# Ten column groups of the input projection as block products, and ten adds moved to GpSimd

## The chip, the cores and the metric

One core of a Trainium2 chip runs one encoder block. The metric is device time in microseconds, the median of the runs shown. Everything is float32; matmuls take operands split into a high and a low part of type fp32r.

## The reference, cut to what matters

```
u = rmsnorm(x, g_mix)                       # x: 512 tokens x 2048
z = u @ W_in                                # 2048 x 6720 columns
qa, ka, va, cq, ckv, kr, ga, gb = split(z)  # 1024, 256, 256, 512, 512, 64, 2048, 2048
qa, ka: rmsnorm per head of 128, rotary; oa = softmax(qa ka^T / sqrt(128)) va; ya = oa @ w_a_out
latent branch from cq, ckv, kr: yb = ob @ w_b_out
h = x + (sigmoid(ga) * ya + sigmoid(gb) * yb) @ w_o
h += (silu(g) * u') @ w_down, [g, u'] = rmsnorm(h) @ w_gate_up
h += sigmoid(rmsnorm(h) @ w_ple_gate) * rmsnorm(p @ w_ple_proj); final rmsnorm
```

## The kernel before, in words

Activations lie with the feature on the partition and 512 tokens along the row. A matmul in full accuracy is three: high weights with high x, high weights with low x, low weights with high x (`product`). A *piece* (`piece`, L649) is 512 rows of a weight matrix by 256 columns: 1024 elements on a partition. SyncE loads it into one of four `raw` buffers (`load`, L390), ScalarE copies it to `w_hi` (`whi`, L1072, behind the use of the piece two before), VectorE subtracts to get `w_lo` (`wlo`, L1651), and TensorE runs 16 matmuls with the high part (L658) and 8 with the low part (L663). Four pieces are a *column group*, 256 columns of z: two 128x512 results in two PSUM banks, which VectorE scales by 1/rms of x while it empties them (`empty`, L1679, 128x1024).

Each engine has its own program, and each works strictly in the order written; the engines meet at semaphores. In the order of TensorE: the group of the keys (while x arrives), the group of the values with the total of the squares of x behind its second piece (`first_total`, L756), the four pieces of the rotary key (L762, 32 matmuls instead of 96), four groups of queries (the chains of two keys and the first query run beside the last three: square, total over the partitions with a matmul of ones, logarithm and exponential, a Newton step, gain, rotation, split), and then eight grouped-query heads.

The squares of x: ScalarE squares tile s into one of two buffers (`x_square`), VectorE adds it to `acc` (`x_add`, L1785), for s = 0 to 15, around the splits of pieces 4 and 5. Then ScalarE splits piece 6, copies the high part of the sum (`sum_split`), VectorE makes the low part (`sum_low`, L1720).

A head on TensorE (`gqa_head`, L784): scores (12 matmuls), two pieces of a gate group, the total of squares of the query three heads on (`head_total`), two pieces, transposes of the probabilities, four pieces of a second gate group with the weighing of the values between them. On ScalarE (L1221): table load, four exponentials, the square of the next query, splits of weight pieces, root, copies, and twice `gate_sigmoid` (L1208: sigmoid of a gate group and its store to DRAM). On VectorE (L1851): maxima, sums and scaling of the probabilities, low parts, norm and rotation of the query, emptying of the gate groups. The last head has two groups of the latent branch instead.

Later, the feed-forward part computes with 2x2 block products (`strassen`, L943): a *unit* is a product of a weight block with x by seven products of half size instead of eight. VectorE and one accumulating DMA make the sums of weight blocks, ScalarE snapshots intermediate banks between them. Units go in pairs, their products alternate. In a *wide* unit the products of high weights with high and low x are one matmul of 512 elements into two half banks, added up later (`folds`); in a *narrow* one they are two of 256. Per product: 8 (or 16) high matmuls (L977; L979 and L980) and 8 low ones of 256 (L983).

Of the kernel before, what the change touches and what calls it, by code (L numbers as in the profile page):

```python
# [25 lines left out]
F32 = mybir.dt.float32  # L26
# [32 lines left out]
N_QKV, N_KR, N_GATE = 0, 8, 28  # L59
N_LAT = N_GATE + 8 * 7  # L60
# [8 lines left out]
G_GATE = 7  # L69
G_LAT = G_GATE + 14  # L70
# [9 lines left out]
UNITS = FF + 24  # L80
A11, A21, A22, A12 = range(4)
# [52 lines left out]
def raw_count(v, i):  # L134

    return 16 * (v // 2) if raw_slot(v, i) in (4, 6) else 16 if v < 2 else 16 * (v // 2 + 1)
# [26 lines left out]

G_MIX, G_FFN, G_PLEN, G_POST, G_FIN, G_QA, G_KVA, G_QN, G_KN = 0, 16, 32, 48, 64, 80, 84, 88, 89
# [7 lines left out]
def build(nc, xT, pT, gains, tables, mats, w_in, w_qb, w_kvb, w_a, w_b, w_o, w_gu, w_dn, w_dn6, w_pg, w_pp,  # L172
          outT):
    with ExitStack() as ctx:
# [37 lines left out]
        sb("between", [P, 20, 2, SEQ])  # L212
# [7 lines left out]
        h_dram = nc.dram_tensor("h_dram", [KD, P, SEQ], F32, kind="Internal").ap()  # L220
        hid = nc.dram_tensor("hid", [3, 8, P, 8, 256], F32, kind="Internal").ap()
# [46 lines left out]
        kr_parts = sem("kr_parts")  # L268

# [30 lines left out]
        SQ_PARTS = r3[:, 7]  # L300
# [42 lines left out]
        X_HALF = [slice(0, 256), slice(256, 512)]  # L343

# [44 lines left out]
        def _(sp):  # L389
# [19 lines left out]
            n = 4  # L409
            for col in [C_V, C_KR, C_Q, C_Q + 256, C_Q + 512, C_Q + 768]:  # L410
                for j in range(4):
                    load(n + j, j, w_in, 4 * j, col)
                if n == 4:
                    sp.dma_start(tab[:], tables).then_inc(tables_in, 16)
                n += 4
            with sp.Fori(0, HEADS - 1) as h:
                ca, cb = sp.snap(h * COLS + C_GA), sp.snap(h * COLS + C_GB)
                for j in range(8):
                    load(h * 8 + N_GATE + j, j % 4, w_in, 4 * (j % 4), ca if j < 4 else cb)
# [37 lines left out]
            sp.wait_ge(gate_out[0], 16 * HEADS)  # L457
# [27 lines left out]
            sp.wait_ge(gate_out[1], 16 * HEADS)  # L485
# [154 lines left out]
        def _(pe):  # L640
# [43 lines left out]
            def head_total(m):  # L684
                pe.wait_ge(hsq_lo, m + 1)
                mm(ps[:, 7, :], ones_r[:], SQ_PARTS[:, 0, :], start=True, stop=False)
                mm(ps[:, 7, :], ones_r[:], SQ_PARTS[:, 1, :], start=False, stop=True).then_inc(htot, 1)

# [49 lines left out]
            def in_group(g, after=None, tiles=2):  # L738

                free(g)  # L740
                for j in range(4):
                    def tile_ready(k, j=j):
                        pe.wait_ge(u_lo, 4 * j + k + 1)

                    piece(4 * g + j, j, 2 * (g % 2), u_pieces(j), j == 0, j == 3, tiles,
                          tile_ready if g == 0 else None)
                    for step in (after or {}).get(j, []):
                        step()
# [13 lines left out]
            def rotary_key_group():  # L762
                free(2)
                for j in range(4):
                    pe.wait_ge(w_lo_done, N_KR + j + 1)
                    for k in range(4):
                        x, w = u_tile(4 * j + k), w_hi[:, j % HL, 0, k]
                        first, last = j == 0 and k == 0, j == 3 and k == 3
                        if last:
                            mm(ps[LOWER, 0, :], w[:, LOWER], x[:, 1, :], start=False, stop=False)  # L770
                        i = mm(ps[:, 0, :], w[:, 0:P], x[:, 0, :], start=first, stop=last)
                        if not last:
                            i = mm(ps[LOWER, 0, :], w[:, LOWER], x[:, 1, :], start=False, stop=False)
# [3 lines left out]
            in_group(3)  # L777
            pe.wait_ge(rstd_done, 1)
            in_group(4, {0: [lambda: head_total(0)], 3: [lambda: turn_v(res[:, 10, :], 4)]})
            in_group(5, {0: [lambda: head_total(1)], 3: [lambda: turn_v(res[:, 11, :], 5)]})  # L780
            in_group(6, {0: [lambda: head_total(2)]})


            def gqa_head(h, kv, more):  # L784
                b = h * 8 + N_GATE
                score(h, [Q_A], [K_A[kv]], h + 5)
                free(h * 2 + G_GATE)
                piece(b, 0, 2, u_pieces(0), True, False)
                piece(b + 1, 1, 2, u_pieces(1), False, False)
                if more:  # L790
                    pe.wait_ge(exp_done, h * 4 + 4)
                    head_total(h + 3)
                piece(b + 2, 2, 2, u_pieces(2), False, False)
                piece(b + 3, 3, 2, u_pieces(3), False, True)
                turn_p(h, 0, PT_BANK)
                turn_p(h, 1, PT_BANK)
                free(h * 2 + G_GATE + 1)
                piece(b + 4, 4, 0, u_pieces(0), True, False)
                weigh(h, 0, V_A[kv], PT_A)
                if more:  # L800
                    pe.wait_ge(hnorm, h + 4)
                turn_p(h, 2, PT_BANK)
                turn_p(h, 3, PT_BANK)
                piece(b + 5, 5, 0, u_pieces(1), False, False)
                weigh(h, 1, V_A[kv], PT_A)
                weigh(h, 2, V_A[kv], PT_A)
                weigh(h, 3, V_A[kv], PT_A)
                piece(b + 6, 6, 0, u_pieces(2), False, False)
                piece(b + 7, 7, 0, u_pieces(3), False, True)
# [4 lines left out]
            with pe.Fori(GROUP, HEADS - 1) as h:  # L814
                gqa_head(h, 1, True)
            gqa_head(HEADS - 1, 1, False)
# [251 lines left out]
        def _(act):  # L1068
# [3 lines left out]
            def whi(n, j):  # L1072
# [3 lines left out]
                if isinstance(n, int) and n >= LAST:  # L1076
                    act.wait_ge(piece_used, N_E + 4)
                    copy(as_piece(LAST_HI[j]), raw[:, j]).then_inc(w_hi_done, 1)
                    return
                if isinstance(n, int) and n == N_WO + 31:  # L1080
# [32 lines left out]
            def head_square(m, tile, need, count):  # L1113
                act.wait_ge(need, count)
                nc.scalar.activation(res[:, 13:14, :], tile, ACT.Square).then_inc(hsq, 1)
                act.wait_ge(hsq, m + 1)
                copy(SQ_PARTS[:, 0:1, :], res[:, 13:14, :]).then_inc(hsq_hi, 1)
# [1522 lines left out]
```

## Time and profile before

| | us |
|---|---|
| median of 3 runs (2668.5 to 2668.79) | 2668.55 |
| profiled execution, whole | 2669.43 |
| span of its instructions | 2667.6 |
| TensorE busy | 2650.6 |
| VectorE busy | 1906.9 |
| ScalarE busy | 1220.6 |
| GpSimd busy | 169.7 |

The span reaches from the first to the last instruction. Busy time is the union of an engine's instructions; a matmul's end is modelled, so neighbours overlap and the distance from start to start is the price of one.

### The profile page before, as it was taken

The numbers are of one execution on the slowest core, as the hardware profiler recorded it, in microseconds if no ns is written. First come the engines' busy times: TensorE is split into PE (matmuls) and PEld (weight loads), VectorE is DVE, ScalarE is ACT, GpSimd is POOL, SyncE is SP. The second block draws the span as 40 slices with busy tenths as digits, with TensorE's granted clock in tenths as the row PEclk, the third lists the DMA queues.
The fourth block names the chain that finished last, engine by engine and source line by source line (L and its number), as shares of the span: only waits on it lengthen the run. The fifth ranks groups of instructions, "written<-read, shape, count | busy, mean of one in ns | idle before, by whom it ended". The sixth has DMA issues, their size and how long they took to land. (4 is left out here: it accounts for less than half of the span.)

```text
span 2667.6 us, 37022 instructions
## 1 busy us (share of the span) xinstructions
PE 2650.6 (99%) x14596; PEld 2304.4 (86%) x14596; DVE 1906.9 (71%) x2192; ACT 1220.6 (46%) x1527; POOL 169.7 (6%) x130
## 2 busy tenths in 40 slices
PE   9999999999999999999999999999999999999998
PEld 7888888888888888898888888888899899999887
DVE  6555555455665433488998999998999898898745
ACT  5334344333554323355545545554555353454543
POOL 0000000010000111100000000000000000000052
PEclk9999999999999999999999999999999999999999
DMA  6333333333233454455455556545557654643332
GB/s 224 95 92 100 109 103 102 103 87 114 90 112 95 174 216 125 140 147 169 141 167 174 151 166 180 166 143 174 174 183 236 197 202 146 206 134 109 95 103 95
DMA packets 130434, 382.62 MB, mean 143 GB/s; under 512 B 11120, under 2 KB 37872, under 8 KB 127728
## 3 DMA queue, kind: packets, MB, share of 16 engines
q1 hardware_dynamic: 113824, 333.35, 37.7%
q0 software_dynamic: 9792, 34.61, 7.4%
q10 hardware_dynamic: 6672, 12.63, 1.2%
q8 instruction: 101, 1.65, 0.3%
q14 instruction: 45, 0.37, 0.0%
HBM read 301.90 MB, written 44.04 MB: 130 GB/s over the span
## 5 line engine op out<-in xcount | busy, mean ns | idle before, releaser
L1070 ACT ACTIVATE w_hi<-raw 128x1024 fp32r<-128x1024 f32 (+1 forms) x533 | 556.9, 1045 | 891.6 <-PE ps L663 447.0
L658 PE MATMUL ps<-arena,w_hi 128*128 128x512 f32 x3344 | 798.5, 390 | 0.4 <-DVE arena L1724 0.4
L658 PEld LDWEIGHTS ps<-arena,w_hi 128*128 128x128 f32 x3344 | 625.1, 188 | 133.0 <-issue 4.2
L1670 DVE TENSOR_TENSOR w_lo<-raw,w_hi 128x1024 fp32r<-128x1024 f32 x212 | 268.1, 1265 | 432.9 <-ACT w_hi L1070 432.4
L977 PE MATMUL ps<-arena,w_hi 128*128 128x512 f32 x1792 | 449.0, 392 | 0.5 <-DVE res L2248 0.5
L2060 DVE TENSOR_TENSOR w_lo<-raw,w_hi 128x1024 fp32r<-128x1024 f32 (+1 forms) x315 | 374.8, 1190 | 80.9 <-ACT w_hi L1070 79.3
L663 PE MATMUL ps<-arena,w_lo 128*128 128x512 f32 x1672 | 413.3, 389 | 0.0
L977 PEld LDWEIGHTS ps<-arena,w_hi 128*128 128x128 f32 x1792 | 322.2, 189 | 58.6 <-DVE res L2248 0.9
L663 PEld LDWEIGHTS ps<-arena,w_lo 128*128 128x128 f32 x1672 | 313.9, 188 | 65.1
L983 PEld LDWEIGHTS ps<-arena,w_lo 128*128 128x128 f32 x2468 | 332.3, 191 | 17.5
L983 PE MATMUL ps<-arena,w_lo 128*128 128x256 f32 x2468 | 346.3, 282 | 0.0
L1070 ACT ACTIVATE hi<-raw 128x1024 fp32r<-128x1024 f32 (+1 forms) x159 | 164.9, 1037 | 212.0 <-PE ps L983 207.9
L977 PE MATMUL ps<-arena,hi 128*128 128x512 f32 x896 | 224.4, 392 | 0.0
L2060 DVE TENSOR_TENSOR lo<-raw,hi 128x1024 fp32r<-128x1024 f32 (+1 forms) x157 | 187.0, 1191 | 41.3 <-ACT hi L1070 40.5
L977 PEld LDWEIGHTS ps<-arena,hi 128*128 128x128 f32 x896 | 161.1, 189 | 28.8
L983 PEld LDWEIGHTS ps<-arena,lo 128*128 128x128 f32 x1228 | 165.4, 191 | 8.7
L983 PE MATMUL ps<-arena,lo 128*128 128x256 f32 x1228 | 172.3, 282 | 0.0
L979 PE MATMUL ps<-arena,w_hi 128*128 128x256 f32 x676 | 166.3, 283 | 0.2 <-ACT res L1070 0.2
L980 PE MATMUL ps<-arena,w_hi 128*128 128x256 f32 x676 | 166.2, 283 | 0.0
L2510 POOL DMA_DIRECT2D raw<-raw x68 | 59.1, 869 | 1220.4 <-DMA raw<-w_gu 785.6
L979 PEld LDWEIGHTS ps<-arena,w_hi 128*128 128x128 f32 x676 | 129.7, 192 | 0.5 <-ACT res L1070 0.4
L980 PEld LDWEIGHTS ps<-arena,w_hi 128*128 128x128 f32 x676 | 129.8, 192 | 0.1
(206 smaller groups left out, 2645.4 us busy)
## 6 DMA issues: line engine op xcount, KB each, us to landing
raw<-w_gu SPq DMA_DIRECT2D x174, 512.0 KB, 4.1
raw<-w_in SPq DMA_DIRECT2D x108, 512.0 KB, 3.5
raw<-w_dn SPq DMA_DIRECT2D x64, 512.0 KB, 4.6
raw<-raw POOLq DMA_DIRECT2D x60, 512.0 KB, 7.3
hid<-res SPq DMA_DIRECT2D x22, 1024.0 KB, 4.8
raw<-w_o SPq DMA_DIRECT2D x32, 512.0 KB, 3.6
raw<-w_pg SPq DMA_DIRECT2D x32, 512.0 KB, 3.6
arena<-hid SPq DMA_DIRECT2D x14, 1024.0 KB, 8.3
```

Of the source, the lines that this page charges most:

```text
L658: mm(ps[:, bank + t, :], w_hi[:, s, t, k], x[:, part, :], start=first and k == 0 and part == 0, stop=False)
L663: i = mm(ps[:, bank + t, :], w_lo[:, s, t, k], x[:, 0, :], start=False, stop=last and k == len(xs) - 1)
L977: mm(parts, w, x[:, :, k], start=fresh and k == 0, stop=False, skip_group_check=not fresh)
L979: mm(out, w, x[:, 0, k], start=fresh and k == 0, stop=False, skip_group_check=not fresh)
L980: mm(out, w, x[:, 1, k], start=False, stop=False, skip_group_check=not fresh)
L983: i = mm(out, lo[:, k * P:k * P + P], x[:, 0, k], start=False, stop=k == pairs(v) - 1, skip_group_check=not fresh)
L1070: return nc.scalar.activation(out, in_, ACT.Copy, scale=scale)
L1670: tt(w_lo[:, j % HL], raw[:, j], w_hi[:, j % HL], ALU.subtract).then_inc(w_lo_done, 1)
L2060: tt(S_LO[s][:, columns(v)], operand(v, j), S_HI[s][:, columns(v)], ALU.subtract).then_inc(s_lo, 1)
L2510: pool.dma_start(RAWS[into][:, columns(v)], RAWS[more][:, columns(v)], accum_op=ALU.add).then_inc(sum_1_in[v % 2], 16)
```

## The change

Ten of the column groups (queries 4 to 7, gate A's first, gate B's first seven) become ten units of block products, between the rotary key and the rest. Two query groups follow (the seam, `N_SEAM`), then the heads with one group each: six of gate A in heads 0 to 5, the latent ones in heads 6 and 7. Units 0, 1, 8, 9 are narrow, 2 to 7 wide. The results of the units go to DRAM (`q_dram`, `gates`), as do the keys, values and the rotary key (`kv_dram`) until the seam. The four turned operands of x (T1 to T4) are made in `res` by VectorE from gained copies of x by ScalarE.

GpSimd adds the squares 6 to 15, and issues the ten accumulating DMAs of the units.

```diff
-N_QKV, N_KR, N_GATE = 0, 8, 28
-N_LAT = N_GATE + 8 * 7
+N_QKV, N_KR, N_SEAM, N_GATE = 0, 8, 12, 20
+N_LAT = N_GATE + 4 * 6
+Z_UNITS = 10
+def z_wide(v):
+    return 0 < v // 2 < Z_UNITS // 2 - 1
@@ tensor @@
             rotary_key_group()
-            in_group(3) ... in_group(6, {0: [lambda: head_total(2)]})
+            def z_product(v, j):
...
+                if j >= 4:
+                    pe.wait_ge(z_snap, snap_at(v, j - 4))
+                pe.wait_ge(z_hi, n + 1)
...
+            for a in range(0, Z_UNITS, 2):
+                for j in range(7):
+                    z_product(a, j)
+                    z_product(a + 1, j)
+            in_group(G_SEAM, {0: [first_seam_step], 2: [lambda: head_total(1)],
+                              3: [lambda: turn_v(res[:, 3, :], 5)]}, N_SEAM, 6)
+            in_group(G_SEAM + 1, {0: [lambda: head_total(2)]}, N_SEAM + 4, 2)
+            def gqa_head(h, kv, more, bank=2):
+                b = h * 4 + N_GATE
                 score(h, [Q_A], [K_A[kv]], h + 5)
+                pe.wait_ge(emptied, h + G_GATE)
+                piece(b, 0, bank, u_pieces(0), True, False)
                 if more:
                     head_total(h + 3)
+                piece(b + 1, 1, bank, u_pieces(1), False, False)
                 turn_p(h, 0, PT_BANK)
                 turn_p(h, 1, PT_BANK)
+                piece(b + 2, 2, bank, u_pieces(2), False, False)
                 weigh(h, 0, V_A[kv], PT_A)
                 turn_p(h, 2, PT_BANK)
                 turn_p(h, 3, PT_BANK)
                 weigh(h, 1, V_A[kv], PT_A)
+                piece(b + 3, 3, bank, u_pieces(3), False, True, before=last_weighs)
@@ scalar @@
             whi(5, 1)
             for k in range(11, 16):
                 x_square(k)
+            for k in range(8):
+                x_scale(k)
             whi(6, 2)
             sum_split(0)
             whi(7, 3)
             root(0, 7, 0, D)
+            z_turned_hi(T1_, 0, 1)
+            z_turned_hi(T1_, 1, 1)
+            for k in range(8, 16):
+                x_scale(k)
             whi(8, 0)
+            z_part(0)
             whi(9, 1)
+            nc.scalar.preload_act_table(ACT.Sigmoid)
...
+                for t in range(14):
+                    if 14 * q + t + 2 < 7 * Z_UNITS:
+                        z_part(14 * q + t + 2)
+                    if q == 0 and t in (7, 8):
+                        z_turned_hi(T3_, t - 7, 7)
...
+                    if t == 8:
+                        z_snap_s1(b)
+                        z_snap_row(b)
...
             def gqa_head(h, kv, more, latent=None):
                 ln_exp_table()
                 exps(h)
                 if more:
                     head_square(h + 3, res[:, bass.ds(h + 1, 1), :], hnorm, h + 3)
...
                 o_split(h, r3[:, bass.ds(h, 1), 0, :])
+                whi(b + 5, 1)
+                if latent is None:
+                    gate_sigmoid(h, 0)
@@ vector @@
             wlo(4, 0)
-            for s in range(6, 11):
-                x_add(s)
             wlo(5, 1)
-            for s in range(11, 16):
-                x_add(s)
+            z_t1(0)
+            z_t1(1)
...
             empty(K_KEPT, 0, 0, 3)
+            z_turned_low(T1_, 1)
             wlo(8, 0)
+            z_t2(0)
+            z_t2(1)
+            z_t4(0)
             wlo(9, 1)
             empty(V_KEPT, 2, 0, 7)
+            z_low(0)
             wlo(10, 2)
             wlo(11, 3)
...
+                        if t == 7:
+                            z_t3(0)
+                            z_t3(1)
...
                 o_split(h, r3[:, bass.ds(h, 1)])
+                if latent is None:
+                    gate_group(h, b + 3)
+                wlo(b + 5, 1)
@@ gpsimd @@
+            for s in range(6, 16):
+                add_square(s, 0, 0, sq_a)
+            for v in range(Z_UNITS):
+                into, more = z_slot(v, A21), z_slot(v, A22)
...
+                pool.dma_start(RAWS[into], RAWS[more], accum_op=ALU.add).then_inc(sum_1_in[v % 2], 16)
```

`x_scale(k)` copies tile k of x times its gain onto itself; `z_turned_hi` copies half of a turned operand (128x1024) to its high part; `z_part(n)` and `z_low(n)` split the weights of product n, a block of 128x1024; `z_snap_s1` copies a unit's first bank; `z_t1` to `z_t4` subtract parts of x (128x1024). The unit's products are numbered n = 14q + t, even t for the even unit of pair q.

## Rows read from the trace of the kernel before

**Rows 1.** The page, busy shares and 40 slices.
```profile
PE 2650.6 (99%) x14596; PEld 2304.4 (86%) x14596; DVE 1906.9 (71%) x2192; ACT 1220.6 (46%) x1527; POOL 169.7 (6%) x130
...
PE   9999999999999999999999999999999999999998
...
PEclk9999999999999999999999999999999999999999
```
**Rows 2.** Waits of TensorE: who waited for whom, us in total, times, longest.
```profile
PE ps L1056 <- ACT tab L1630: 2.2, 1, 2.2
```
**Rows 3.** Timeline of TensorE, first 110 us: start, length, instructions.
```profile
40.96 0.39 PE L681 MATMUL ps<-sum_r,ones_r 128*128 128x512 f32 x1
...
52.29 0.39 PE L771 MATMUL ps<-arena,w_hi 128*128 128x512 f32 x1
...
59.86 3.79 PE L658 MATMUL ps<-arena,w_hi 128*128 128x512 f32 x16
...
65.30 3.79 PE L658 MATMUL ps<-arena,w_hi 128*128 128x512 f32 x16
```
**Rows 4.** Chain that ended last, feed-forward part: start, us, what (wide, then narrow).
```profile
2096.53 1.84 PE ps L977 x8
...
2099.32 1.84 PE ps L977 x8
...
2140.52 0.96 PE ps L983 x8
...
2143.40 0.96 PE ps L983 x8
```
**Rows 5.** Timeline of ScalarE, first 110 us.
```profile
6.34 2.56 ACT L1070 ACTIVATE arena<-res,gn 128x512 fp32r<-128x512 f32 x4 [0.28 <-DMA res<-xT]
...
35.80 1.06 ACT L1070 ACTIVATE w_hi<-raw 128x1024 fp32r<-128x1024 f32 x1 [0.20 <-PE ps L663]
36.77 0.61 ACT L1070 ACTIVATE sum_r<-acc 128x512 fp32r<-128x512 f32 x1
```
**Rows 6.** Timeline of GpSimd, adds of squares: alone, and beside VectorE.
```profile
1043.97 2.72 POOL L2491 TENSOR_TENSOR acc<-acc,tab 128x512 f32<-128x512 f32 x2 [19.04 <-ACT tab L1096]
...
563.09 3.42 POOL L2491 TENSOR_TENSOR acc<-acc,tmp 128x512 f32<-128x512 f32 x2 [23.02 <-ACT tmp L1096]
```
**Rows 7.** Timeline of VectorE, first 110 us.
```profile
26.32 1.22 DVE L1670 TENSOR_TENSOR w_lo<-raw,w_hi 128x1024 fp32r<-128x1024 f32 x1
27.46 3.87 DVE L1792 TENSOR_TENSOR acc<-acc,tmp 128x512 f32<-128x512 f32 x5
...
38.17 0.69 DVE L1720 TENSOR_TENSOR sum_r<-acc,sum_r 128x512 fp32r<-128x512 f32 x1
```
**Rows 8.** Timeline of TensorE, head 2: first score, total of squares.
```profile
251.69 0.39 PE L645 MATMUL ps<-arena 128*128 128x512 f32 x1
...
265.29 0.39 PE L686 MATMUL ps<-arena,ones_r 128*128 128x512 f32 x1
```
**Rows 9.** Timeline of ScalarE, head 2.
```profile
251.95 1.06 ACT L1070 ACTIVATE w_hi<-raw 128x1024 fp32r<-128x1024 f32 x1 [4.44 <-PE ps L663]
255.44 1.06 ACT L1212 ACTIVATE tmp<-tmp 128x1024 f32<-128x1024 f32 x1 [2.43 <-DVE tmp L1682]
...
258.79 0.69 ACT L1138 ACTIVATE res<-ps,negmax 128x512 f32<-128x512 f32 x1
...
261.46 0.65 ACT L1115 ACTIVATE res<-res 128x512 f32 x1
...
282.65 1.28 ACT L1212 ACT_TABLE_LOAD   x1
```
**Rows 10.** Timeline of VectorE, head 2.
```profile
262.80 0.69 DVE L1728 TENSOR_TENSOR arena<-res,arena 128x512 fp32r<-128x512 f32 x1 [0.50 <-ACT arena L1070]
```
**Rows 11.** Busy time by stretch, the clock behind POOL's; then TensorE's first matmuls.
```profile
2655.00:2656.00 1.00, 0.66 (x2) 0.48 (x2) 0.61 (x1) 1.00 (x3) 0.00 (x0) 0.70 0.25 83
...
1.47 6.33 PE L753 MATMUL ps<-arena 128*128 128x512 f32 x16 [1.47 <-DVE arena L1781]
```

More of the change, by code:

```diff
@@ L68 @@
 N_END = N_PLE + 32
-G_GATE = 7
-G_LAT = G_GATE + 14
+G_SEAM = 3
+G_GATE = G_SEAM + 2
+G_LAT = G_GATE + 6
 G_FIRST_B = G_LAT + 5
@@ L299, in build @@
         P_IN = emb[:, 6:8, :]
-        SQ_PARTS = r3[:, 7]
+        K_KEPT, V_KEPT, KR_KEPT = (between[:, i] for i in range(3))
         SUM_PARTS = [sum_r[:]] * 5 + [arena[:, 14]]
@@ L408, in _ @@
             sp.dma_start(cm[:], mats).then_inc(mats_in, 16)
-            n = 4
-            for col in [C_V, C_KR, C_Q, C_Q + 256, C_Q + 512, C_Q + 768]:
-                for j in range(4):
[L412 to L419, printed above, removed]
+            for j in range(4):
+                load(4 + j, j, w_in, 4 * j, C_V)
@@ new lines, in _, with kept @@
+            for i in (A11, A21, A22):
+                z_load(0, i)
+            for j in range(4):
+                load(N_KR + j, j, w_in, 4 * j, C_KR)
+            for i in (A11, A21, A22):
+                z_load(1, i)
+            for v in range(2):
+                z_load(v, A12)
+            def kept(first, last):
+                return kv_dram[first:last].rearrange("k p s -> p k s")
+            sp.wait_ge(emptied, 2)
+            sp.dma_start(kept(0, 2), K_KEPT).then_inc(kv_out, 16)
+            sp.dma_start(kept(2, 4), V_KEPT).then_inc(kv_out, 16)
@@ new lines, in _ @@
+            sp.wait_ge(emptied, 3)
+            sp.dma_start(kept(4, 5), KR_KEPT[:, 0:1]).then_inc(kr_out, 16)
+            for a in range(2, Z_UNITS, 2):
+                for i in (A21, A22, A11, A12):
+                    z_load(a, i)
+                    z_load(a + 1, i)
+            a, b = Z_UNITS - 2, Z_UNITS - 1
+            sp.wait_ge(z_sum, sum_at(b, SUM_4))
+            sp.wait_ge(z_lo, order(b, 4) + 1)
+            load(N_SEAM, 0, w_in, 0, C_Q)
+            sp.wait_ge(kv_out, 32)
+            sp.wait_ge(z_out[2], 32 * 2)
@@ new lines, in _ @@
+            for j in range(4):
+                load(N_SEAM + 4 + j, j, w_in, 4 * j, C_Q + COLS)
+            sp.wait_ge(kr_out, 16)
+            sp.wait_ge(z_out[1], 32 * 3)
+            sp.dma_start(res[:, 12:13, :], kept(4, 5)).then_inc(kr_in, 16)
+            for j in range(4):
+                load(N_GATE + j, j, w_in, 4 * j, C_GA + COLS)
+            sp.wait_ge(op_lo, OP_Q + 1)
+            sp.wait_ge(z_out[0], 32)
+            sp.dma_start(res[:, 4:8, :], q_dram.rearrange("k p s -> p k s")).then_inc(q_in, 16)
@@ L420, in _ @@
+            with sp.Fori(1, HEADS - 2) as h:
+                ca = sp.snap(h * COLS + (C_GA + COLS))
+                for j in range(4):
+                    load(h * 4 + N_GATE + j, j, w_in, 4 * j, ca)
             for g in range(4):
@@ L736, in u_pieces, with in_group @@
                 return [u_tile(4 * j + k) for k in range(4)]
-            def in_group(g, after=None, tiles=2):
-                free(g)
+            def in_group(g, after=None, n=None, bank=None):
                 for j in range(4):
@@ new lines, in z_snap_s2, with z_store @@
+            def z_snap_s2(u):
+                act.wait_ge(z_used, order(u, 4) + 1)
+                copy(z_rows(u)[:, 1, z_taken(u)], ps[:, bank0(u) + ALPHA, z_taken(u)]).then_inc(z_snap, 1)
+            def z_store(u):
+                rows = z_rows(u)[:, :, LEFT]
+                act.wait_ge(z_scaled, 2 * u + 2)
+                if u >= 2:
+                    nc.scalar.activation(rows, rows, ACT.Sigmoid).then_inc(z_sig, 1)
+                    act.wait_ge(z_sig, u - 1)
+                for k in range(2):
+                    act.dma_start(z_result(u)[k].rearrange("p (t c) -> p t c", t=2),
+                                  rows[:, 2 * k:2 * k + 2]).then_inc(z_out[u % 4], 16)
@@ L1180, in _ @@
                 x_square(k)
+            for k in range(8):
+                x_scale(k)
             act.wait_ge(set_done, 1)
```

579 lines of the change are left out of this document (441 added, 138 removed).

## The prediction

> **What bounds the kernel now.** I read the page's busy shares and slices first. TensorE is busy 99% of the span and in tenths of 9 in every slice but the last, at full granted clock [rows 1]. Then TensorE's waits: the longest of the whole run is 2.2 us, near the end [rows 2]. So TensorE's stream of matmuls sets the time from about 8 us on, and every other engine counts only where it arrives after TensorE. The change must therefore be read twice: what it takes out of the stream, and where it makes the stream wait. For the second I read the timelines of TensorE, ScalarE and VectorE over the first 110 us and over one grouped-query head (251 to 303 us).
>
> **Taken out of the stream.** A piece of 24 matmuls takes 65.30 - 59.86 = 5.44 us [rows 3], a group of four pieces 21.76, ten groups 217.6 us. The feed-forward part already runs the block products that take their place. A wide one takes 2099.32 - 2096.53 = 2.79 us, a narrow one 2143.40 - 2140.52 = 2.88 [rows 4]. Units 2 to 7 are wide, 0, 1, 8, 9 narrow: 6 x 7 x 2.79 + 4 x 7 x 2.88 = 197.8. **Saved: 19.8 us** if TensorE never waits. All that follows is what it waits.
>
> **The first total.** TensorE comes to the total of squares of x at 40.96 [rows 3]; the sum's low part was ready at 38.86 [rows 7], 2.1 us earlier. Now ten of the sixteen adds are GpSimd's. Two adds of this kind take 2.72 us, with the semaphore between them, so one more per 1.43 us [rows 6]; VectorE made five in 3.87 [rows 7]. Squares have two buffers, so square s waits for add s-2 and the loop goes at GpSimd's pace: the first add starts at about 26.6, as the piece's split starts at 26.32 just behind the last of VectorE's adds [rows 7], add 13 ends at 26.6 + 8 x 1.43 = 38.0, square 15 ends at 38.6. Behind it ScalarE now has eight gain copies, 2.56 / 4 = 0.64 each by the nearest kind [rows 5], 5.1 us at most (4.2 at the 0.52 of a plain one): 43.5. Then the split of piece 6 (0.97 from its start to the next, [rows 5]), while VectorE waits to follow it with 1.14 [rows 7]; the total's low part stands behind that with 0.7. Ready at 46.4. **First wait: 5.4 us.** Bounds: 4.5 with short copies, 8 with slow adds. VectorE gains 7.7 us of its own here, but they were not on the path.
>
> In rows two GpSimd adds took 3.42 instead of 2.72 where VectorE worked on two operands beside them [rows 6]. The Trainium skill (SBUF — State Buffer, "SBUF: two separate sides") says that a VectorE instruction with two SBUF inputs and a GpSimd one take a shared port pair exclusively, each for its whole length; the trace's 3.42 agrees. By that rule the adds come at the slower pace wherever VectorE is busy beside them, which is the rival of that name below; by the uncontended row they don't, and the sum takes that, because VectorE has only two low parts in this stretch.
>
> **The rotary key's pieces.** Its four pieces took 59.86 - 52.29 = 7.57 us [rows 3], too short to cover much. ScalarE has before them two turned copies (0.97 each) and eight more gain copies (5.1), VectorE the low half of T1 twice, the reciprocal, the emptying of the key, T2 twice and half of T4, at 1.14 a 128x1024 operation. In order: total done 47.0, root and turned copies to 50.4, gain copies to 55.2, split of piece 8 to 56.2; VectorE's T2 and T4 end at 60.1, so the low half of piece 9 is there at 60.4 where TensorE wants it at 59.6; then the value's emptying, the first block's low part, piece 10 at 63.1 where it is wanted at 62.4. **1.6 us.** The four pieces end at 66.9 instead of 59.86.
>
> **The first pair of units.** VectorE still has the rotary key (2.85 us), T4 low twice and two block low parts; the second product waits 0.5 us for its low weights. From there VectorE runs back to back: sixteen operations of 1.14 from 74.5 to the first half of T3 at 92.8. ScalarE stands waiting for that half (it is asked for before the next split), then copies it, splits block 10, copies the second half (0.97 each) and only then takes the snapshot of the odd unit's first bank, which TensorE's tenth product waits for: about 96.3, against 66.9 + 0.5 + 9 x 2.88 = 93.3. **3.0 us.** Bounds 0 (the waits before it give the same time back) and 6 (the second accumulating DMA lands late). The following units have VectorE 14 low parts, 6 weight sums and 4 sums of 1.14 and 8 operations of half size per 39.1 us, 33 us in all: nothing.
>
> **The seam** between units and heads has two groups for the chain that had three (square, total, root, norm, rotation, split, for two keys and a query). By the same adding up, the second key's total stands 1.4 us behind its place, since ScalarE first stores units 8 and 9, loads a table and then takes the root. **1.4 us,** 0 to 4.
>
> **The heads.** A head now has four pieces instead of eight. It costs no time by itself (29.5 us of matmuls), but the total of the next query's squares moves up: it was behind two pieces, 265.29 - 251.69 = 13.60 us after the head's first score [rows 8]; now it is behind one, at 13.60 - 5.44 = 8.16. What it needs is a chain on ScalarE and VectorE. After the last head's last piece ScalarE splits a piece (start 251.95, 0.26 after the score's start), then has that head's gate. The gate's sigmoid started at 255.44, waiting for VectorE; the exponentials start 3.35 us after it (store issue and table load between), the head's square 2.67 later, the low part of the square 1.34 after that [rows 9, 10]. In the changed order the emptying stands ahead of the piece's low part, so the sigmoid no longer waits for it; but with one gate a head, each sigmoid has its own table load before it, 1.28 as at 282.65 [rows 9]. So: 0.26 + 0.97 + 1.28 = 2.5; + 3.35 + 2.67 + 1.34 = 9.9; + 0.69 = 10.55 us after the score's start. TensorE stands there from 8.16: 2.4 us. Before, the same low part was ready at 11.8 and wanted at 13.6. The wait comes in heads 1 to 6 (head 0 has no gate before it, head 7 no next query). **14.4 us.** Bounds: 0, and 6 x 3.7 = 22 if the sigmoid is as late as it was. The later steps fit: weighing 0 wants its operand 6.3 us after the second piece and gets it after 5.9.
>
> **The clock.** After TensorE's wait of 2.2 us, from 2653 on [rows 2], the granted clock was 0.70 in the next microsecond [rows 11]. The 16 first matmuls took 6.33 us instead of 16 x 0.227 = 3.6 [rows 11], 2.7 lost. The change makes seven waits of 2.4 to 3.0 us (the wait of 5.4 is followed by one that would take its loss). Between 0 and 7 x 2.7 = 19 us; a wait can itself hold part of the slow time, so I take half of the waits at half the price: **4.7 us.**
>
> **Sum:** -19.8 + 5.4 + 1.6 + 0.5 + 3.0 + 1.4 + 14.4 + 4.7 = +11.2. Against the profiled execution (span 2667.6, 2669.43 around it) 2680.6; the median of the runs is 0.9 lower, so **2680 us**.
>
> **Rivals.**
> - *All covered.* Only the stream counts: 2668.5 - 19.8 = 2649. For it: VectorE is busy 71%, ScalarE 46% as a whole. Against it: the order of the queues above. Chance 0.10.
> - *The head's chain is shorter than I add up* (the sigmoid's table load sits earlier, in ScalarE's idle time). Without any head wait and with little clock loss 2668.5 - 19.8 + 11.9 + 1 = 2662; with the table load alone gone, 6 x 1.1 us remain and it is 2669. With a head wait of w the time is 2661.6 + 6w, so this mechanism makes the kernel faster than before by more than 0.2% from w under 0.3 us. Against it: in the trace the load of 282.65 stands right before its sigmoid in the queue, behind the head's copies [rows 9]. Chance 0.20, half to each.
> - *GpSimd stretches.* At 1.8 us an add the first total comes 8 x 0.37 = 3 us later: 2683. It decides nothing unless VectorE's chain also slips. Chance 0.05.
> - *The clock falls at every wait* and costs its full price: 2680 + 14 = 2694. For it: the one wait of this size in the trace did it. Against: that one followed thinner work. Chance 0.12.
> - *As computed:* 0.53, with its own range 2671 to 2690.
>
> Range over the cases: 2657 to 2695. A difference under 0.2% (2663.2 to 2673.9) can't be told from none: faster 0.17, same 0.18, slower 0.65.
>
> **What would show it.** Right: TensorE idle about 5 us at 41 us; about 3 us in the tenth product of the units; in six heads an idle stretch of 2 to 3 us ahead of the total of squares, with VectorE's low part as its releaser; units at 19.6 and 20.2 us each. Wrong: no idle there and a saving near 19 us; or product times above 2.9; or new waits in the latent attention, which the change leaves alone.

## The result, and the profile after

The changed kernel took 2698.81 us (four runs, 2697.98 to 2700.24), the kernel before beside it 2668.67 (2668.5 to 2669.34): ratio 1.0113, 95% interval 1.0096 to 1.0131. The forecast was 2680, with 2695 as its upper end. The direction was right, the size was not: +30.1 us instead of +11.2.

The head of the page answers to [rows 1]:

```profile
span 2697.3 us, 37937 instructions
PE 2649.1 (98%) x14980; PEld 2318.1 (86%) x14980; DVE 2013.5 (75%) x2300; ACT 1287.3 (48%) x1612; POOL 193.5 (7%) x150
PE   8999999999999999999999999999999999999998
PEclk9999999999999999999999999999999999999999
```

The first thing to see is a number that did not move. 19.8 us of matmuls left the stream, and TensorE's busy time fell only from 2650.6 to 2649.1. So TensorE was busy some 18 us longer with the work that is left. The row of the clock is too coarse for it: every slice still shows a 9, and the mean over the span is 0.992 where it was 0.998.

TensorE's waits, the whole run (who waited for whom: us in total, times, longest), where [rows 2] had 2.2 at the top:

```profile
PE ps L823 <- DVE arena L2025: 15.1, 7, 2.9
PE ps L816 <- DVE sum_r L2016: 7.3, 1, 7.3
PE ps L793 <- ACT w_hi L1253: 4.0, 1, 4.0
PE ps L943 <- ACT res L1253: 2.5, 1, 2.5
PE ps L1239 <- ACT tab L1926: 2.2, 1, 2.2
...
PE ps L943 <- DVE res L2162: 0.8, 1, 0.8
PE ps L941 <- DVE res L2162: 0.7, 1, 0.7
...
PE ps L906 <- DVE w_hi L1957: 0.5, 1, 0.5
PE ps L947 <- DVE w_lo L2132: 0.4, 1, 0.4
```

In this order they are: the total of the next query's squares in six heads (14.5, and 0.6 of the seam), the first total, the first piece of the seam, the units' tenth product, the old wait of 2.2, two waits at unit boundaries, the rotary key, the second product. The new ones make 31.3 us. The forecast had 26.3 for waits and 4.7 for the clock.

The timeline of TensorE (start, length, instructions, and the idle time ahead of them with its releaser): the first total and the pieces behind it, the first of the rotary key's matmuls, the seam, two of the heads, and the mark where the last head's stage ends.

```profile
48.41 0.77 PE L816 MATMUL ps<-sum_r,ones_r 128*128 128x512 f32 x1 [7.32 <-DVE sum_r L2016]
49.40 5.01 PE L793 MATMUL ps<-arena,w_hi 128*128 128x512 f32 x16
...
61.50 0.39 PE L906 MATMUL ps<-arena,w_hi 128*128 128x512 f32 x1
...
278.96 6.28 PE L793 MATMUL ps<-arena,w_hi 128*128 128x512 f32 x16 [4.00 <-ACT w_hi L1253]
...
402.42 0.49 PE L823 MATMUL ps<-arena,ones_r 128*128 128x512 f32 x1 [2.87 <-DVE arena L2025]
...
402.98 5.20 PE L793 MATMUL ps<-arena,w_hi 128*128 128x512 f32 x15
...
470.17 0.49 PE L823 MATMUL ps<-arena,ones_r 128*128 128x512 f32 x1 [2.43 <-DVE arena L2025]
...
470.74 3.80 PE L793 MATMUL ps<-arena,w_hi 128*128 128x512 f32 x16
...
598.84 1.02 PE L811 MATMUL ps<-acc,cm 128*128 128x512 f32 x2
```

Sixteen such matmuls take 3.79 where nothing disturbs them [rows 3]. Behind the wait of the head at 470 they took 3.80; behind the head's at 402 the fifteen of this row took 5.20 and all sixteen 5.43; behind the first total 5.01; at the seam 6.28. The stretches behind the waits, with the granted clock behind POOL's figure:

```profile
402.00:406.00 4.00, 3.58 (x11) 2.83 (x12) 3.49 (x5) 1.83 (x3) 0.00 (x0) 0.69 0.27 49
470.00:474.00 4.00, 3.83 (x17) 3.19 (x18) 3.45 (x6) 1.58 (x3) 0.00 (x0) 1.00 0.31 80
48.00:50.00 2.00, 1.59 (x4) 1.33 (x5) 1.40 (x2) 0.36 (x1) 0.00 (x0) 0.50 0.70 184
```

0.50 is the lower of the two levels, 1.2 GHz of 2.4; 0.69 is a stretch with part of its time at each. The clock fell behind eight of the nine long waits: the first total, the tenth product, the seam and five of the six heads. In the first total and the seam, with waits of 7.3 and 4.0, it was down before the wait ended (0.50 from 45.5 to 48 and from 277.5 to 278.9).

By stages, from the positions of TensorE in both traces ("computed": the kernel before, its pieces replaced by block products and no wait added; the units' 197.8 is the forecast's):

| stage | computed | after | more | of it waits in the list |
|---|---|---|---|---|
| start to rotary key | 52.29 | 61.50 | 9.2 | 7.3 |
| rotary key | 7.57 | 8.24 | 0.7 | 0.5 |
| ten units | 197.8 | 205.1 | 7.3 | 4.4 |
| seam | 45.8 | 53.4 | 7.6 | 4.6 |
| eight heads | 246.2 | 270.6 | 24.4 | 14.5 |
| sum | | | 49.1 | 31.3 |

The first head's scores and the mark in the kernel before:

```profile
149.22 0.39 PE L645 MATMUL ps<-arena 128*128 128x512 f32 x1
...
569.52 1.02 PE L676 MATMUL ps<-acc,cm 128*128 128x512 f32 x2
```

So 149.22 - 59.86 - 2 x 21.76 = 45.8 for the seam, 569.52 - 149.22 - 8 x 21.76 = 246.2 for the heads. Less 19.8 the sum is +29.3, and the mark at 598.84 stood at 569.52: +29.3. Behind it the two kernels run alike. Of the 17.8 us that no wait in the list accounts for, slow matmuls are some 14 by the lengths above (1.6 in each of five heads, 2.5 at the seam, 1.6 at the first total, 1.2 of it in the piece and the rest in the total's own matmuls, 1.7 in the units). The rest, some 4 us, goes with the waits' edges: the end of a matmul is modelled, so the list counts each idle stretch some 0.2 to 0.3 us short.

### The profile page after: what moved, and what is told of

Read it like the earlier page. It is cut to its first block and busy times, and to the rows that moved or that the text cites. A ratio compares the mean times of both kernels' runs of the same rounds, so it can differ in the third digit from the quotient of the medians.

```text
span 2697.3 us, 37937 instructions
## 1 busy us (share of the span) xinstructions
PE 2649.1 (98%) x14980; PEld 2318.1 (86%) x14980; DVE 2013.5 (75%) x2300; ACT 1287.3 (48%) x1612; POOL 193.5 (7%) x150
## 5 line engine op out<-in xcount | busy, mean ns | idle before, releaser
L1253 ACT ACTIVATE w_hi<-raw 128x1024 fp32r<-128x1024 f32 (+1 forms) x539 | 562.9, 1045 | 788.3 <-PE ps L1166 412.5
L793 PE MATMUL ps<-arena,w_hi 128*128 128x512 f32 x2704 | 659.1, 396 | 4.0 <-ACT w_hi L1253 4.0
L793 PEld LDWEIGHTS ps<-arena,w_hi 128*128 128x128 f32 x2704 | 513.8, 191 | 116.0 <-issue 7.9
L1160 PE MATMUL ps<-arena,w_hi 128*128 128x512 f32 x1792 | 449.0, 392 | 0.5 <-DVE res L2701 0.5
L1966 DVE TENSOR_TENSOR w_lo<-raw,w_hi 128x1024 fp32r<-128x1024 f32 x172 | 220.1, 1279 | 272.5 <-ACT w_hi L1253 272.1
L1160 PEld LDWEIGHTS ps<-arena,w_hi 128*128 128x128 f32 x1792 | 322.3, 189 | 58.4 <-DVE res L2701 0.7
L1166 PEld LDWEIGHTS ps<-arena,w_lo 128*128 128x128 f32 x2468 | 332.4, 191 | 17.6
L798 PE MATMUL ps<-arena,w_lo 128*128 128x512 f32 x1352 | 334.4, 389 | 0.0
L1253 ACT ACTIVATE hi<-raw 128x1024 fp32r<-128x1024 f32 (+1 forms) x183 | 190.4, 1040 | 252.8 <-PE ps L1166 208.6
L798 PEld LDWEIGHTS ps<-arena,w_lo 128*128 128x128 f32 x1352 | 253.8, 188 | 52.7
L1162 PEld LDWEIGHTS ps<-arena,w_hi 128*128 128x128 f32 x676 | 129.7, 192 | 0.5 <-ACT res L1253 0.4
L1163 PEld LDWEIGHTS ps<-arena,w_hi 128*128 128x128 f32 x676 | 129.8, 192 | 0.1
```

The costliest lines, as they stand in the source:

```text
L793: mm(ps[:, bank + t, :], w_hi[:, s, t, k], x[:, part, :], start=first and k == 0 and part == 0, stop=False)
L798: i = mm(ps[:, bank + t, :], w_lo[:, s, t, k], x[:, 0, :], start=False, stop=last and k == len(xs) - 1)
L1160: mm(parts, w, x[:, :, k], start=fresh and k == 0, stop=False, skip_group_check=not fresh)
L1162: mm(out, w, x[:, 0, k], start=fresh and k == 0, stop=False, skip_group_check=not fresh)
L1163: mm(out, w, x[:, 1, k], start=False, stop=False, skip_group_check=not fresh)
L1166: i = mm(out, lo[:, k * P:k * P + P], x[:, 0, k], start=False, stop=k == pairs(v) - 1, skip_group_check=not fresh)
```

## The experiments

Each edit is to the changed kernel, unless another is named. The kernel before ran beside all of them, at 2668.8 to 2669.0.

**1. The gate behind the square root.** The last head's gate (its table load, sigmoid and store) goes out of the way of the next head's exponentials and square, and is issued behind the root of that square. If the six waits come from it, they go, and what the clock costs there goes with them.

```diff
             def gqa_head(h, kv, more, latent=None, gate=True):
...
+                if gate:
+                    gate_of_last_head(h)
...
-                if latent is None:
-                    gate_sigmoid(h, 0)
-                else:
+                if latent is not None:
```

> The changed kernel with one edit on ScalarE: the sigmoid and store of a head's gate are issued in the next head behind the root of its total of squares, and the table of logarithm and exponential is loaded right behind them. Theory (waits and clock): the chain to the total of squares loses two table loads and the sigmoid, its low part is ready about 8 us after the first score where TensorE wants it at 8.2, so the six waits of 14.5 us go, and with them the five falls of the clock, 1.7 us each: 2698.8 - 14.5 - 8.5 = 2676, and up to 2 us given back at the weighing of the values, since the split of the fourth piece comes 0.4 us later. Rival (the chain only moves: the root's and rotation's chain ends late and TensorE waits at the first weighing instead): 2690 or more, with waits named for the operand of the probabilities.

2678.38 us (2676.62 to 2679.29), ratio 1.0036 (1.0021 to 1.005): 20.4 less than the changed kernel, where 23 was expected. The total in head 1 on TensorE, and the clock over the heads, after the experiment:

```profile
366.78 0.41 PE L823 MATMUL ps<-arena,ones_r 128*128 128x512 f32 x1
...
367.26 3.81 PE L793 MATMUL ps<-arena,w_hi 128*128 128x512 f32 x16
```

```profile
320.00:560.00 240.00, 239.75 (x1114) 197.01 (x1114) 163.17 (x256) 124.87 (x194) 2.18 (x2) 1.00 0.29 90
```

And the same stretch of the changed kernel:

```profile
320.00:560.00 240.00, 225.51 (x1009) 184.75 (x1008) 155.07 (x236) 114.32 (x176) 0.00 (x0) 0.96 0.27 83
```

No wait and no slow stretch is left in the heads. The waits in the list were 14.5; the gate's place on ScalarE costs 20.4. (The seam's wait was 4.6 in this run, not 4.0, and hides some of it; experiment 5 shows what this wait follows.) From the first head's first score to the last head's mark TensorE took 577.66 - 329.12 = 248.5 us, where the changed kernel took 270.6.

**2. The waits filled.** Ten matmuls whose sums nothing reads stand ahead of the total in heads 1 to 6. They take about as long as the wait, so TensorE works instead of standing; the chain that it waits for is as late as ever. What is gained is the clock's alone.

```diff
                 piece(b, 0, bank, u_pieces(0), True, False)
+                if more and not (isinstance(h, int) and h == 0):
+                    for _ in range(10):
+                        mm(ps[:, 1, :], ones_r[:], u_tile(0)[:, 0, :], start=True, stop=True)
```

> The changed kernel with ten extra matmuls of 512 columns (2.27 us) into a PSUM bank that nobody reads, in heads 1 to 6, between the first piece and the total of squares; it computes nothing with them. They fill the wait and leave what ends it where it is. Theory (the falls of the clock are a cost of their own beside the waits): the waits stay as time but TensorE is busy in them, the clock does not fall in the heads, 5 x 1.7 = 8.5 us less: 2690. Rival (the clock's falls there cost nothing, as the next wait takes the time back): 2699, no change. Rival (the matmuls come on top of the wait): 2698.8 + 6 x 2.3 = 2712.

2692.09 us (2691.59 to 2693.57), ratio 1.0087 (1.007 to 1.0104): 6.7 less, with more work; 8.5 was expected.

```profile
369.14 2.43 PE L977 MATMUL ps<-arena,ones_r 128*128 128x512 f32 x10
371.40 0.48 PE L823 MATMUL ps<-arena,ones_r 128*128 128x512 f32 x1
...
371.94 3.81 PE L793 MATMUL ps<-arena,w_hi 128*128 128x512 f32 x16
```

```profile
300.00:560.00 260.00, 258.46 (x1192) 212.96 (x1191) 181.36 (x274) 129.26 (x200) 2.17 (x2) 1.00 0.28 88
```

The filler takes 2.43 where TensorE idled 2.09 in this head, the sixteen matmuls behind it 3.81 where they took 5.43, and the clock stays up through all heads. In this run the seam's wait was 6.5 instead of 4.0, which took part of the gain; the edit stands behind the seam and did not cause it. The heads alone, from the first score to the mark, took 593.97 - 331.48 = 262.5 us: 8.1 less than the 270.6 of the changed kernel, which is five falls at 1.6. The remaining 14.0 down to experiment 1's 248.5 are the late chain's own. This is the direct measurement of the term that the forecast had too small.

**3. The squares' adds back on VectorE.** The ten adds that the change gave to GpSimd go back into VectorE's queue.

```diff
+            for s in range(6, 11):
+                x_add(s)
...
-            for s in range(6, 16):
-                add_square(s, 0, 0, sq_a)
```

> The changed kernel with the ten adds of squares 6 to 15 back on VectorE, as before the change; the eight gain copies stay ahead of the total. Theory: the squares end at 35.6 instead of 40.2, so the first total's wait falls from 7.3 to about 2.8 us; but the rotary key's pieces and the first pair wait for VectorE and ScalarE, whose chain starts 4.5 us earlier as well, so most of the gain holds, and the clock may still fall once: 2694 to 2696. Rival (the adds on GpSimd cost nothing, what counts is the gain copies): within 1 us of 2698.8.

2693.94 us (2693.06 to 2695.29), ratio 1.0095 (1.0078 to 1.0112): 4.9 less. The first wait is 2.6 instead of 7.3, and the rotary key starts 5.0 us earlier. That the whole gain comes out near it is in part chance: the seam waited 5.9 in this run instead of 4.0, and the clock fell in four heads instead of five, which gave 1.6 back.

**4. The gain copies behind the split.** The eight gain copies that stand ahead of the first sum's split go behind it, and on VectorE the making of T1 (`z_t1`) behind the sum's low part.

```diff
-            for k in range(8):
-                x_scale(k)
...
             sum_split(0)
+            for k in range(8):
+                x_scale(k)
             whi(7, 3)
...
-            z_t1(0)
-            z_t1(1)
...
             sum_low(0)
+            z_t1(0)
+            z_t1(1)
```

> The changed kernel with the first eight gain copies of x on ScalarE, and VectorE's T1 made from them, behind the split of the sum of squares instead of ahead of the split of piece 6; the adds stay with GpSimd. Theory: the total is ready at about 43.2 instead of 48.3, a wait of 2.2 us instead of 7.3. But the chain through T1, T2 and T4 is no shorter, so the rotary key's pieces and the first pair wait more: of the 5 us, 1 to 3 come back there; 2694 to 2697. Rival (the first wait is all there is): 2698.8 - 5.1 - 2 (a fall of the clock) = 2692.

2700.30 us (2699.44 to 2700.43), ratio 1.0118 (1.0102 to 1.0135): 1.5 more, with ranges that overlap, where 2694 to 2697 was expected. A miss. The first wait did shrink, from 7.3 to 3.2, but the sixteen matmuls behind the total took 6.22 where they had taken 5.01, and the rotary key's pieces waited 1.9 instead of 0.5, so that the units began only 1.3 us earlier. The seam then waited 6.0 instead of 4.0; experiments 1 and 2 show 4.6 and 6.5 there with nothing changed ahead of it, so this is not shown to come from the copies. From TensorE's waits of this run:

```profile
PE ps L793 <- ACT w_hi L1253: 6.0, 1, 6.0
PE ps L816 <- DVE sum_r L2016: 3.2, 1, 3.2
...
PE ps L906 <- DVE w_hi L1957: 1.9, 2, 1.5
```

ScalarE has the same copies to make before the rotary key wherever they stand. Putting them behind moved most of the wait; it did not remove it.

**5. The seam and the tenth product.** ScalarE's split of the seam's first piece goes ahead of its wait for the first key, and the copies of T3 behind the snapshots.

```diff
-                    if q == 0 and t in (7, 8):
-                        z_turned_hi(T3_, t - 7, 7)
...
+                    if q == 0 and t in (8, 9):
+                        z_turned_hi(T3_, t - 8, 7)
...
+            whi(N_SEAM, 0)
             act.wait_ge(k0_in, 16)
             head_square(0, res[:, 0:1, :], z_out[3], 32 * 2)
-            whi(N_SEAM, 0)
```

> The changed kernel with two orders on ScalarE changed: the split of the seam's first piece ahead of the wait for the first key's row (which stands behind the stores of units 6 and 7), and the high parts of T3 in the first pair behind the snapshots of units 0 and 1. Theory: both waits were ScalarE standing at a semaphore with ready work behind it. The wait of 4.0 us at the seam and of 2.5 us in the tenth product go, with their falls of the clock (1.7 and about 3 us): 2698.8 - 11 = 2687 to 2688. Rival (the pieces or the stores are late themselves, the transfers set the seam): the first wait moves to the total of squares or to piece 13, and 2693 or more is left.

2695.38 us (2692.66 to 2697.22), ratio 1.0098 (1.0081 to 1.0115): 3.4 less, where 11 was expected. The tenth product no longer waits and the first piece of the seam neither, but two totals behind it now do:

```profile
278.87 0.50 PE L823 MATMUL ps<-arena,ones_r 128*128 128x512 f32 x1 [3.04 <-DVE res L2162]
...
294.73 0.79 PE L823 MATMUL ps<-arena,ones_r 128*128 128x512 f32 x1 [3.79 <-DVE arena L2025]
```

4.0 at the first piece became 3.0 and 3.8 at the totals. The seam is bound by a chain on ScalarE and VectorE that ends at the two keys' totals; the split was only the first place where TensorE met it. The changed kernel's ScalarE there:

```profile
276.58 0.63 ACT L1301 ACTIVATE res<-res 128x512 f32<-128x512 f32 x1 [8.36 <-DMA gates<-res]
...
277.78 1.99 ACT L1253 ACTIVATE w_hi<-raw 128x1024 fp32r<-128x1024 f32 x2
```

It stands 8.36 us for a DMA, and the split that TensorE needs is behind it. The DMA is the store of unit 7 (`z_out[3]` in the edit above), and the square of the first key is written over that unit's rows. ScalarE issued its two halves at 265.85 and 266.43; it was complete at 276.5, 10.1 us later, where the median of these stores is 5.0. The first key itself had been in since 265.4. In experiments 1 to 4 the same store took 10.7, 12.6, 12.0 and 12.1 us, and the seam's first piece waited 4.6, 6.5, 5.9 and 6.0: the wait follows the store, also where the edit changes nothing ahead of it. Three loads of weight pieces were issued behind it, and the DMA engines' mean share was 0.90 from 266 to 276; whether that made the store slow no run shows.

**6 and 7. All four orders, with the adds on VectorE and on GpSimd.** Experiments 1, 4 and 5 together, once with experiment 3 and once without it. The pair gives the adds' price where nothing else of this is late.

```diff
 # 7 against 6
-            for s in range(6, 11):
-                x_add(s)
...
+            for s in range(6, 16):
+                add_square(s, 0, 0, sq_a)
```

> All edits so far on the changed kernel: gate behind the root, adds on VectorE, first gain copies behind the sum's split, seam and T3 orders. Theory (only waits and their clock stood between the block products and their 19.8 us): no wait at the first total; about 3 us of waits in the rotary key's pieces, since T1, T2 and T4 now start later relative to them; 0 to 1 in the first pair, 1 to 2 at the seam, 1.3 in the units: 2668.8 - 19.8 + 7 + 3 for the clock = 2659, faster than the kernel before. Rival (the time comes back elsewhere, in attention or in DMA): 2668 or more.

> As the run with all edits, but the ten adds stay on GpSimd. Theory: the squares end at 40.2 instead of 35.6, the total is ready at 43.2 where TensorE wants it at 41: 2 to 3 us of wait and one fall of the clock, of which the rotary key's waits give back some: 2 to 5 us above that run, 2661 to 2664. Rival (with the other orders mended the adds are covered): the same time.

With VectorE 2665.66 us, ratio 0.999 (0.998 to 0.9999); with GpSimd 2670.99, ratio 1.0009 (1.0 to 1.0019). The price of the adds on GpSimd is 5.3 (2 to 5 was expected), and they alone decide whether the whole comes out just below the kernel before or just above it. The first of the two missed its 2659 by 6.7, and with it the second its 2661 to 2664: the rotary key waited 2.4 and the seam 0.9 and 3.85, the last with a slow stretch behind it.

**8. The order around the rotary key**, from experiment 6: VectorE's T2 and T4 and its low parts are interleaved as their pieces want them, and the second product's split and low part go ahead of T4's.

```diff
             z_t2(0)
-            z_t2(1)
-            z_t4(0)
             wlo(9, 1)
-            empty(V_KEPT, 2, 0, 7)
-            z_low(0)
+            z_t2(1)
             wlo(10, 2)
+            z_t4(0)
             wlo(11, 3)
+            z_low(0)
+            empty(V_KEPT, 2, 0, 7)
```

> As the run with all edits and the adds on VectorE, and VectorE's three operations T2, T2, T4 stand one by one between the low parts of pieces 8 to 11 instead of all ahead of piece 9; the low part of the second product stands ahead of T4's, on ScalarE its split ahead of T4's high part. Theory: the rotary key's waits fall from about 3 us to under 1, and the second product's 0.4 us goes: 2 to 3 us less than that run. Rival (ScalarE's sixteen gain copies set this stretch, not VectorE's order): no change.

2664.05 us, ratio 0.998 (0.9971 to 0.999), 1.6 less than 6, where 2 to 3 was expected. The rotary key's waits fell from 2.4 to 0.5, and in the profiled execution the units began 2.0 us earlier. The seam took most of that back: its first total waited 1.5 instead of 0.9, and the sixteen matmuls behind the second took 6.02 instead of 5.41.

**9. Two totals of the seam later**, from experiment 8: the second key's and the next query's total one piece later in TensorE's stream, where their chain is done.

```diff
-            in_group(G_SEAM, {0: [first_seam_step], 2: [lambda: head_total(1)],
-                              3: [lambda: turn_v(res[:, 3, :], 5)]}, N_SEAM, 6)
-            in_group(G_SEAM + 1, {0: [lambda: head_total(2)]}, N_SEAM + 4, 2)
+            in_group(G_SEAM, {0: [first_seam_step],
+                              3: [lambda: turn_v(res[:, 3, :], 5), lambda: head_total(1)]}, N_SEAM, 6)
+            in_group(G_SEAM + 1, {1: [lambda: head_total(2)]}, N_SEAM + 4, 2)
```

> As the run with all edits and the rotary key's order, and in the seam the totals of squares of the second key and the first query stand one piece later on TensorE. Theory: the 3.9 us wait for the second key's low part and the fall of the clock behind it (1.7 to 3.4 us) go; VectorE's low part of the seam's sixth piece comes 0.7 us late: 2664.0 - 5 = 2659, some 0.35% below the kernel before. Rival (the chain of keys and query ends later and TensorE waits at the first scores instead): 2663 to 2664, with a wait there.

2661.04 us (2660.49 to 2662.52) against 2668.97, ratio 0.9972 (0.9961 to 0.9984). It is 2 us short of the expected 2659, and below both kernels: 0.3% under the kernel before. The seam's waits in its timeline:

```profile
268.89 0.50 PE L823 MATMUL ps<-arena,ones_r 128*128 128x512 f32 x1 [1.36 <-DVE res L2172]
...
281.71 3.92 PE L793 MATMUL ps<-arena,w_hi 128*128 128x512 f32 x16 [0.75 <-ACT w_hi L1253]
...
298.72 2.11 PE L798 MATMUL ps<-arena,w_lo 128*128 128x512 f32 x8 [1.26 <-DVE w_lo L1976]
```

Its mean clock is that of before, 0.998, and the last head's mark is at 560.52, 9.0 us ahead of 569.52.

**10. The kernel before with the ten adds on GpSimd**, and nothing else of the change.

```diff
-            for s in range(6, 11):
-                x_add(s)
...
+            for s in range(6, 16):
+                add_square(s, 0, 0, sq_a)
```

> The kernel before with one part of the change alone: the ten adds of squares 6 to 15 on GpSimd. Theory: at 1.43 us an add and more where VectorE works beside it, the total is ready 4.6 us later than 38.9, at 43.4 to 43.8, where TensorE wants it at 41.0: 2.5 us of wait, and a fall of the clock behind it for 1.7 to 3.4: 2668.7 + 4.5 = 2673 (2671 to 2675). Nothing behind it gives time back. Rival (2.1 us of cover and a short wait that costs no clock): 2670 to 2671.

2673.61 us (2672.35 to 2674.6), ratio 1.0017 (1.0008 to 1.0026): 4.6 more. GpSimd, then TensorE:

```profile
26.22 15.80 POOL L2487 TENSOR_TENSOR acc<-acc,tmp 128x512 f32<-128x512 f32 x10 [25.77 <-ACT tmp L1096]
```

```profile
43.98 0.77 PE L681 MATMUL ps<-sum_r,ones_r 128*128 128x512 f32 x1 [3.20 <-DVE sum_r L1720]
44.98 4.92 PE L658 MATMUL ps<-arena,w_hi 128*128 128x512 f32 x16
```

A wait of 3.2 where there was none, and 1.1 in the piece behind it: 2673 was expected, for this reason. This half of the change makes the kernel slower by itself.

## Why the prediction was wrong

**The step that failed is the clock.** "I take half of the waits at half the price": 4.7 us. The runs showed eight of nine long waits followed by a slow stretch, five of the six in the heads at 1.6 us of slow matmuls each, for some 14 us in all. That is 9 of the 19 us that the forecast was short; alone it would have made 2689, inside the range. Another 4 us are the waits' edges, which the forecast had no term for, and the rest is in the steps below. Experiment 2 shows the clock apart from the waits: with the stream kept busy and the chain as late as before, the kernel is 6.7 us faster, and its heads 8.1, though it does 6 x 2.43 = 14.6 us of extra matmuls in the place of 14.5 us of waits. The argument for the half was that the one fall in the trace of before "followed thinner work". The heads are dense and the clock fell there all the same. The price of one fall, 2.7, taken from the kernel's first matmuls, was not too low: it was 1.6 in the heads and 2.5 at the seam. I expected falls behind half of the waits, and the price was halved on top; of the two halves the first was plainly wrong (eight of nine), and eight falls at the measured 1.6 to 2.5 make 14. The rival *the clock falls at every wait*, at 0.12 and 2694, had the mechanism. With the first total and the seam put right it gives 2699, but in part by luck: its 19 us at 2.7 a fall are too many for the slow matmuls, and the edges of the waits make up the difference.

**The first total:** 5.4 forecast, 7.3 measured. The order was as written. GpSimd's ten adds, and the sixth of them alone:

```profile
26.54 15.83 POOL L2944 TENSOR_TENSOR acc<-acc,tmp 128x512 f32<-128x512 f32 x10 [26.08 <-ACT tmp L1281]
...
34.55 2.08 POOL L2944 TENSOR_TENSOR acc<-acc,tmp 128x512 f32<-128x512 f32 x1
```

Eight of the ten took 1.3 us, and where one of these was followed by another their starts lay 1.44 apart, as forecast. The first (2.11) and the sixth (2.08) ran beside VectorE's low parts of 26.29 and 33.24, and the add behind each began 2.25 and 2.23 after it: 1.6 us in all, so the last square ended at 40.2 instead of 38.6. ScalarE's eight copies took 4.99, as forecast. Some 0.3 more is VectorE's: the second half of T1 held it until 46.4, a term that the sum did not have. The prediction took the undisturbed pace "because VectorE has only two low parts in this stretch"; these two are what it cost. The rival *GpSimd stretches* had the reason right, but not its extent, 1.8 for every add. Experiments 3, 7 and 10 put this half of the change at 4.9, 5.3 and 4.6 with its clock.

**The seam:** 1.4 forecast, 4.0 and 0.6 measured, with the dearest of the slow stretches (2.5) behind. I placed the wait at the second key's total. It came earlier, at the first piece, whose split stands in ScalarE's queue behind a wait of 8.36 us for the store of unit 7. That a store could land 10 us after its issue was not in the sum. Where I was right, that the chain is late, experiment 5 shows it: with the split taken ahead, the totals wait. The store sets where this chain begins (experiment 5). What share the two engines' queues have in its length was not taken apart.

**The heads:** 14.4 forecast, 14.5 measured, in six heads, with VectorE's low part as releaser, as written. The chain by its steps, in the head whose total waits at 402 (ScalarE, then VectorE):

```profile
391.79 1.06 ACT L1253 ACTIVATE w_hi<-raw 128x1024 fp32r<-128x1024 f32 x1 [2.38 <-PE ps L798]
392.87 1.28 ACT L1513 ACT_TABLE_LOAD   x1
394.17 1.06 ACT L1513 ACTIVATE tmp<-tmp 128x1024 f32<-128x1024 f32 x1
...
396.30 1.28 ACT L1341 ACT_TABLE_LOAD   x1 [1.07 <-issue]
397.59 0.69 ACT L1324 ACTIVATE res<-ps,negmax 128x512 f32<-128x512 f32 x1
...
400.26 0.64 ACT L1301 ACTIVATE res<-res 128x512 f32 x1
```

```profile
401.59 0.69 DVE L2025 TENSOR_TENSOR arena<-res,arena 128x512 fp32r<-128x512 f32 x1 [0.49 <-ACT arena L1253]
```

The table load stands right before its sigmoid, as forecast; exponentials 3.42 behind the sigmoid's start (3.35), the square 2.67 behind them (2.67), the low part 1.33 behind that (1.34). So the rival of a shorter chain was wrong. Experiment 1 shows the cause: the gate out of the way, the waits are gone.

**The smaller terms.** Tenth product 3.0 forecast, 2.5 measured, released by ScalarE's snapshot as written. Rotary key 1.6 forecast, 0.5 measured: it came later by the first wait's extra time, which probably gave its chain slack; experiments 4 and 6, with less of it, show 1.9 and 2.4. Second product 0.5, measured 0.4. Two waits at unit boundaries, 0.8 and 0.7, I had not seen at all. The block products took 2.79 and 2.88, so the saving of 19.8 is right.

**The sum again:** 11.2 + 13.1 for the clock and the edges (17.8 for 4.7) + 1.9 for the first total + 3.2 for the seam + 1.5 for the unit boundaries - 1.1 - 0.5 for the rotary key and the tenth product = 29.3, the difference at the mark.

## What to carry to other kernels

On an engine that sets the time, price a new wait by its length and by the slow matmuls behind it: here five of six waits of 2.1 to 2.9 us cost 1.6 more each, and each wait 0.2 to 0.3 more at its edges. Work that leaves the bound engine's stream is worth only what the other engines' queues can give up at the same place: of 19.8 us removed, the best of these kernels kept 7.9, and only with the adds back on VectorE and the orders of experiments 1, 4, 5, 8 and 9. Before an instruction is given to an idle engine, look whether the engine it leaves was late; VectorE was not, and the idle one was slower. And where a queue waits for a store to land, look up how long after its issue that store landed, in several runs.

## What the runs showed that I had not expected

- *A short wait in dense work lowers the clock, but not each time.* 2.09 us was enough in one head, 2.43 was not in another (granted clock 0.68 and 1.00 behind them). In experiment 3 the same six waits were there, and it was the other way round: 1.00 behind the 2.09, 0.70 behind the 2.43, and 1.00 behind the 2.39 as well. So the length of the wait does not decide it. In experiment 5 a wait of 3.04 was followed by a granted clock of 1.00 and sixteen matmuls in 3.90, while in experiment 6 one of 3.85 was followed by 5.41. What tells them apart stays open.
- *Idle shown and idle lost differ.* The waits in the list came to 31.3 us, the time lost to 49.1.
- *An operation of VectorE beside GpSimd's adds took twice its time:*

```profile
33.24 2.25 DVE L1966 TENSOR_TENSOR w_lo<-raw,w_hi 128x1024 fp32r<-128x1024 f32 x1 [5.73 <-ACT w_hi L1253]
```

Before, it took 1.22 [rows 7]. The Trainium skill (SBUF — State Buffer, "SBUF: two separate sides") says that of a VectorE operation with two inputs in SBUF and a GpSimd one, the one that starts first holds a shared port pair for its whole instruction, and the other stands. The trace agrees: the operation of 33.24 began within the add of 33.11 (1.29 us) and took 2.25, and the add of 34.55 began within that operation and took 2.08.
